# A two-block transformer kernel: the first block's activations are projected without the norm's factor per token

## The reference, cut to what matters

```
def rms_norm(x, g, eps=EPS):
    y = xf * lax.rsqrt(jnp.mean(xf * xf, axis=-1, keepdims=True) + eps)
    return y * g

h = rms_norm(x, norm_g[i])
proj = h @ w_in[i]
dq, dk, dv, dg, mq, mk, mv, mg, gates = split_in_proj(proj)
dq = partial_rope(dq, cos, sin);  dk, mq, mk likewise
o_a = diff_attention(dq, dk, dv, ...) * silu(dg)
o_b = moba_attention(mq, mk, mv) * silu(mg)
merged = sigmoid(g_a) * (o_a @ w_branch_diff) + sigmoid(g_b) * (o_b @ w_branch_moba)
```

## Time and profile before

| | |
|---|---|
| median of 3 runs | 1220.8 us (1220.32 to 1221.1) |
| the profiled execution's own time | 1220.15 us |
| its span (first to last instruction) | 1218.3 us |
| TensorE busy | 1186.1 us, 97% |
| VectorE, ScalarE, GpSimd busy | 911.3, 782.4, 417.3 us |
| mean granted TensorE clock | 0.997 of full |
| chain of waits by engine | PE 79%, POOL 9%, DVE 5%, issue 4%, ACT 3% |

### The profile page before, as it was taken

How to read it: one execution, slowest core, us unless ns; L and a number is a source line. 1 busy time by engine, 2 the same in 40 slices (tenths; PEclk the granted TensorE clock), 3 DMA queues, 4 the chain that set the end, 5 groups by cost and what they waited for, 6 DMA issues and landing times.

```text
span 1218.3 us, 26657 instructions
## 1 busy us (share of the span) xinstructions
PE 1186.1 (97%) x8256; PEld 1068.5 (88%) x8256; DVE 911.3 (75%) x1992; ACT 782.4 (64%) x1784; POOL 417.3 (34%) x398
## 2 busy tenths in 40 slices
PE   8999999999898999999999999999999999999997
PEld 8898988989787999888999999998888888888886
DVE  5788778889677769996788788851776768686766
ACT  5546676556775565667788878776655555555555
POOL 2230110011241049998777777789000000000000
PEclk9999999999999999999999999999999999999999
DMA  6787756549543446555666666667676676767663
GB/s 241 231 280 269 229 173 213 183 135 342 193 142 117 141 146 186 188 189 169 204 210 202 212 203 215 211 212 266 195 256 205 207 238 196 254 191 260 197 194 105
DMA packets 85829, 249.86 MB, mean 205 GB/s; under 512 B 8020, under 2 KB 29693, under 8 KB 84989
## 3 DMA queue, kind: packets, MB, share of 16 engines
q1 hardware_dynamic: 77356, 209.62, 54.3%
q0 software_dynamic: 8400, 39.34, 9.1%
HBM read 237.38 MB, written 13.12 MB: 206 GB/s over the span
## 4 chain that ended last, share of the span: by engine, by line
PE 79%; POOL 9%; DVE 5%; issue 4%; ACT 3%; POOLq 0%; DVEq 0%; ACTq 0%
PE psum L704 78%; POOL w_lo L1654 9%; DVE w_lo L1830 1%; ACT w_hi L1227 1%; PE psum L905 1%; ACT arena L1386 1%; DVE rstd L1824 1%; DVE h_parts L1879 0%; ACT arena L1210 0%; DVE arena L2044 0%; DVE arena L1950 0%; POOLq L1653 0%; ACT L1386 0%; DVE arena L2411 0%; DVE s_sb L1844 0%
## 5 line engine op out<-in xcount | busy, mean ns | idle before, releaser
L704 PE MATMUL psum<-h_parts,w_hi 128*128 128x256 f32 (+1 forms) x3216 | 673.9, 303 | 13.5 <-DVE h_parts L1879 4.4
L1227 ACT ACTIVATE w_hi<-ring 128x512 fp32r<-128x512 f32 x734 | 445.1, 627 | 247.9 <-PE psum L704 237.5
L704 PEld LDWEIGHTS psum<-h_parts,w_hi 128*128 128x128 f32 x3216 | 515.2, 191 | 47.5 <-issue 17.8
L704 PE MATMUL psum<-h_parts,w_lo 128*128 128x256 f32 x1832 | 517.1, 282 | 0.0
L1654 POOL TENSOR_TENSOR w_lo<-ring,w_hi 128x512 fp32r<-128x512 f32 x261 | 342.1, 1326 | 147.6 <-ACT w_hi L1227 139.2
L704 PEld LDWEIGHTS psum<-h_parts,w_lo 128*128 128x128 f32 x1832 | 349.9, 191 | 0.0
L704 PE MATMUL psum<-w_hi,h_parts 128*128 128x512 f32 (+1 forms) x1120 | 342.6, 388 | 0.2
L1830 DVE TENSOR_TENSOR w_lo<-ring,w_hi 128x512 fp32r<-128x512 f32 x345 | 229.3, 689 | 77.9 <-ACT w_hi L1227 77.3
L704 PEld LDWEIGHTS psum<-w_hi,h_parts 128*128 128x128 f32 x1120 | 208.6, 188 | 44.8 <-issue 3.0
L704 PE MATMUL psum<-w_lo,h_parts 128*128 128x512 f32 (+1 forms) x560 | 216.4, 386 | 0.0
L2362 DVE TENSOR_TENSOR w_lo<-ring,w_hi 128x512 fp32r<-128x512 f32 x128 | 88.5, 692 | 61.6 <-ACT w_hi L1227 58.1
(11 more groups left out here) (214 smaller groups left out, 1001.8 us busy)
## 6 DMA issues: line engine op xcount, KB each, us to landing
ring<-u_t SPq DMA_DIRECT2D x128, 512.0 KB, 3.6
ring<-v_rows SPq DMA_DIRECT2D x128, 512.0 KB, 4.2
ring<-weights SPq DMA_DIRECT2D x115, 512.0 KB, 4.3
arena<-mods POOLq DMA_DIRECT2D x48, 512.0 KB, 5.6
routing_weights<-s_sb SPq DMA_DIRECT2D x32, 320.0 KB, 4.2
s_sb<-routing_weights POOLq DMA_DIRECT2D x5, 2048.0 KB, 10.0
bias_rows<-bias_row POOLq DMA_DIRECT2D x1, 1536.0 KB, 11.2
xres<-x_t SPq DMA_DIRECT2D x2, 512.0 KB, 4.6
```

Of the source, the lines that this page charges most:

```text
L704: return nc.tensor.matmul(out, lhs, rhs, start=start, stop=stop, **kw)
L1227: nc.scalar.activation(w_hi[:, half, :], src, ACT.Copy).then_inc(hi_done, 1)
```

## The change

The activation parts are now made from x * gain alone, without rstd. So they need neither the sum of squares nor the reciprocal. Everything that is linear in the token's factor takes it later:

- **Start.** SP first issues a DMA for the 8 columns of norm gains, then x. VectorE makes `h_hi` of chunks 0 to 3 (a tensor_scalar) and `h_lo` of all 8 (scalar_tensor_tensor: x * gain - h_hi); ScalarE makes `h_hi` of chunks 4 to 7, after all four halves of `w_hi`. VectorE now also makes `w_lo` of dq1's first half, which GpSimd did. The 14 matmuls of ones after the sum are gone. TensorE does dq0 and dq1 by halves: dq0 over chunks 0 to 3, dq1 over 0 to 3, dq0 over 4 to 7, dq1 over 4 to 7.
- **Rotation.** VectorE multiplies cos and sin by rstd once; GpSimd's cos products wait for that.
- **Values.** Tokens are on partitions there, so the factor is needed as a column: at dv TensorE turns rstd with two matmuls (128 x 128 stationary, one column moving), VectorE copies the two columns out, and the four evictions become tensor_scalar with that column.
- **Gates.** GpSimd multiplies each of the 24 gate blocks by rstd in place, one block behind the projection; ScalarE's silu and sigmoid wait for it.

```diff
+            gains = slice(*PAR["norm_g"])
+            sp.dma_start(par[:, gains], params[:, gains]).then_inc(gain_in, 16)
             for i in range(2):
                 sp.dma_start(xres[:, 4 * i:4 * i + 4, :], x_t[:, 4 * i:4 * i + 4, :]).then_inc(x_in[i], 16)
...
                         sum_squares(AT[s + ("ssq",)], blk(SQ, 8), KC, lambda c: pe_.wait_ge(squared, c + 1))
-                        for _ in range(14):
-                            mm(psum[:, 7, 0:P], ones[:, :], ones[:, :], True, True)
...
+                    if s[1] == "dv":
+                        pe_.wait_ge(rstd_ready, 1)
+                        for i in range(TT):
+                            last = mm(psum[:, 7, T + i:T + i + 1], rstd[:, P * i:P * i + P], ident[:, 0:1], True, True)
+                        last.then_inc(token_done, 1)
...
-                    if s[1] in ("dq0", "nq0"):
+                    if s[1] == "dq0":
+                        outs, k = [take_a(AT[s] + j) for j in range(2)], SPLIT[SLOT_AT[s]]
+                        for b in range(2):
+                            for j in range(2):
+                                half = half_ready(k + j, b)
+                                for c in range(4 * b, 4 * b + 4):
+                                    pe_.wait_ge(h_ready, c + 1)
+                                    last = split_mms(outs[j], half, c % 4 * P, (h_hi[:, c, :], h_lo[:, c, :]), c == 0, c == KC - 1)
+                                last.then_inc(a_done if b else half_used, 1)
...
                     if k == 0:
-                        highs(0)
+                        highs(1)
+                        act.wait_ge(gain_in, 16)
+                        for c in range(DVE_PARTS, KC):
+                            nc.scalar.activation(h_hi[:, c, :], xres[:, c, :], ACT.Copy, scale=pcol("norm_g", c))\
+                                .then_inc(late_hi, 1)
...
+            def scale_gate(b):
+                pool.wait_ge(a_read, filled("proj", FILL1[b]))
+                dst = blk(SIL + b) if b < 8 else blk(SIG + b - 8)
+                nc.gpsimd.tensor_tensor(dst, dst, rstd[:, :], ALU.mult).then_inc(gate_scaled, 1)
...
                 while k_lo <= ahead(s):
-                    if k_lo == 1:
-                        pool.wait_ge(lo0_done, 1)
-                        low(1, 2, ring[:, 1, 0:HSLOT], 3, lo0_done)
                     second_half(k_lo)
                     k_lo += 1
+                if kind == "proj" and s[1] in FILL1[1:]:
+                    scale_gate(FILL1.index(s[1]) - 1)
+                elif kind == "ple":
+                    scale_gate(len(FILL1) - 1)
...
+            def low_start(c):
+                v.scalar_tensor_tensor(h_lo[:, c, :], xres[:, c, :], pcol("norm_g", c), h_hi[:, c, :].bitcast(F32),
+                                       ALU.mult, ALU.subtract).then_inc(h_ready, 1)
...
                     if k == 0:
-                        lows(0)
+                        dve.wait_ge(gain_in, 16)
+                        dve.wait_ge(x_in[0], 16)
+                        for c in range(DVE_PARTS + 1):
+                            if c == 4:
+                                dve.wait_ge(x_in[1], 16)
+                            if c < DVE_PARTS:
+                                v.tensor_scalar(h_hi[:, c, :], xres[:, c, :], pcol("norm_g", c), None, ALU.mult)\
+                                    .then_inc(start_hi, 1)
+                            if c:
+                                dve.wait_ge(start_hi, c)
+                                low_start(c - 1)
+                        low(0, ring[:, 0, 0:HSLOT], 1, lo0_done)
+                        low(2, ring[:, 1, 0:HSLOT], 3, lo0_done)
+                        k_lo = 2
+                        for c in range(DVE_PARTS, KC):
+                            dve.wait_ge(late_hi, c - DVE_PARTS + 1)
+                            low_start(c)
...
+                            dve.wait_ge(small_in, 16 * 8)
+                            for table in (cos_t, sin_t):
+                                v.tensor_tensor(table, table, rstd[:, :], ALU.mult).then_inc(table_scaled, 1)
+                            dve.wait_ge(table_scaled, 2)
...
+                    if s[1] == "dv":
+                        dve.wait_ge(token_done, 1)
+                        v.tensor_copy(token_rstd, psum[:, 7, T:T + TT]).then_inc(token_ready, 1)
+                        dve.wait_ge(token_ready, 1)
                     for i in range(TT):
                         n = VT[s + (i,)]
                         dve.wait_ge(v_done, n + 1)
-                        v.tensor_copy(rows[:, i, :], vbank(n)).then_inc(v_read, 1)
+                        v.tensor_scalar(rows[:, i, :], vbank(n), token_rstd[:, i:i + 1], None, ALU.mult).then_inc(v_read, 1)
```

More of the change, by code:

```diff
@@ L62 @@
 V_MODS = 4
+DVE_PARTS = 4
 MODS_A, MODS_O, MODS_B, MODS_C = 23, 26, 34, 40
@@ L282, in block_program @@
         gain_sum = blk(OT)
+        token_rstd = small[:, 48:48 + TT]
         gain_sq, gain_both = small[:, 32:40], small[:, 40:48]
@@ L376, in block_program @@
         th_done = sem("th_done")
+        gain_in = sem("gain_in")
+        start_hi = sem("start_hi")
+        late_hi = sem("late_hi")
+        table_scaled = sem("table_scaled")
+        token_done = sem("token_done")
+        token_ready = sem("token_ready")
+        gate_scaled = sem("gate_scaled")
         part_hi = sem("part_hi")
@@ L618, in _ @@
             load_slot(1)
-            sp.dma_start(par[:, :], params).then_inc(par_in, 16)
+            sp.dma_start(par[:, gains.stop:NPAR], params[:, gains.stop:NPAR]).then_inc(par_in, 16)
             for name, dst in (("ident", ident[:, :]), ("iota", iota[:, :]), ("valid", valid[:, :]),
@@ L1332, in _ @@
                     highs(ahead(s))
-                    first = {0: 0, 2: 8, 3: 16}[k]
-                    for c in range(KC):
+                    first = {0: 0, 2: 0, 3: 8}[k]
+                    for c in range(KC if k else 0):
                         act.wait_ge(t_ready, first + c + 1)
-                        if c == 0 and k:
+                        if c == 0:
                             act.wait_ge(*((a_done, filled("gate", 7)) if k == 2 else (v_done, VT["out2", 7] + 1)))
-                        t = blk(NTMP[k] + c)
-                        if k:
-                            sh = (0 if k == 2 else 24) + c
-                            nc.scalar.activation(h_hi[:, c, :], t, ACT.Identity, bias=mod[:, sh:sh + 1]).then_inc(th_done, 1)
-                        else:
-                            nc.scalar.activation(h_hi[:, c, :], t, ACT.Copy).then_inc(th_done, 1)
+                        sh = (0 if k == 2 else 24) + c
+                        nc.scalar.activation(h_hi[:, c, :], blk(NTMP[k] + c), ACT.Identity, bias=mod[:, sh:sh + 1])\
+                            .then_inc(th_done, 1)
                 elif s == ("x1", 0):
@@ L1940, in _ @@
                         if k == 0:
+                            dve.wait_ge(small_in, 16 * 8)
+                            for table in (cos_t, sin_t):
+                                v.tensor_tensor(table, table, rstd[:, :], ALU.mult).then_inc(table_scaled, 1)
+                            dve.wait_ge(table_scaled, 2)
                             dve.wait_ge(par_in, 16)
-                            k_lo = 2
                         lows(ahead(s))
-                    first = {0: 0, 2: 8, 3: 16}[k]
-                    for c in range(KC + 1):
+                    first = {0: 0, 2: 0, 3: 8}[k]
+                    for c in range(KC + 1 if k else 0):
                         if c < KC:
                             t = blk(NTMP[k] + c)
-                            gain = {0: pcol("norm_g", c), 2: gain_both[:, c:c + 1], 3: gm[:, 1, c:c + 1]}[k]
+                            gain = {2: gain_both[:, c:c + 1], 3: gm[:, 1, c:c + 1]}[k]
                             src = blk(MERGED + c) if k == 2 else xres[:, c, :]
```

18 lines of the change are left out of this document (9 added, 9 removed).

## The result

The changed kernel is slower, not faster. Its median is 1223.95 us (7 runs, 1222.69 to 1226.13) against 1220.8 us before; the ratio is 1.0023 (95% interval 1.0014 to 1.0032). Its profiled execution took 1223.29 us with a span of 1221.4, 3.1 us more than before. Forecast were 1217.1 us and a ratio under 1.

The account below looks back on a forecast made before the run. TensorE, busy 97% of the span, bounds the kernel, with waits at the start. Start -4.5, turning matmuls +0.45, evictions 0, gate products +0.4 sum to -3.65 us: 1217.1 us, forecast 1216.0 to 1218.4 (8-in-10 range 1215.0 to 1219.8).

Parts of the forecast that it names:

- step 4 of the start: Start: VectorE's first w_lo done at 9.57 us, squares summed by 9.4, so dq0 starts at about 9.65 instead of 13.85.
- the start's gain: Start up to dq2: dq2 begins at 17.3 to 17.8 us instead of 22.00, 4.5 us earlier, bounds 3.4 and 5.3.
- Step 1: Start: SyncE's one added DMA issue costs 0.45 us, so x lands at 5.4 us.
- Only about 0.3 us lie between the sum and dq0: Start: TensorE's remaining wait after the sum of squares, so the 14 removed matmuls of ones are not needed.
- The gate products: 24 products on GpSimd hold up VectorE, unhidden only at the attention stage's end: +0.4 us, bounds 0 and 2.2.
- A hold of that size is hidden there: Attention stage, 97 to 117 us: VectorE held 0.2 us, at most 0.74, by a gate product costs TensorE nothing.
- The slower rival: Attention stage, 97 to 188 us: gate products set VectorE's pace, 0.3 us each, 7.2 in all, so 1224; chance 6%.
- The clock rival: At 188.99 us: gates lengthen TensorE's 1.56 us wait to 2 and the clock falls, +1.5, so 1218.7; chance 6%.
- the value evictions: Behind the start: four evictions become tensor_scalar, difference 0, bounds -0.3 to +0.3 us in all.
- the turning matmuls: At dv: two added matmuls on a full TensorE, +0.45 us, bounds 0.25 and 0.93.
- VectorE's and GpSimd's hold on each other: Start, step 5: one GpSimd instruction holds VectorE up to 1.0 us; late h_lo end at 13.9, reciprocal starts then.
- the point to compare at: dq2's start, 22.00 us before: what it gains, everything behind inherits unless a new wait gives it back.

Follow-up runs that it names:

- a1: After, with norm 0's sum of squares in a PSUM bank of its own: 1219.85 us, ratio 0.9989 to the kernel before.
- a4: After, with the sum of squares in its own bank and 8 matmuls of ones before ple's third block: 1218.34 us, ratio 0.9977.
- a2: After without the 24 gate products on GpSimd: 1221.18 us, ratio 0.9995 to the kernel before.
- a3: After, with 8 matmuls of ones while TensorE waits for ple's third projection: 1222.06 us, ratio 0.9998.
- c2: After, with 11 matmuls of ones ahead of dq0: 1222.11 us, ratio 1.0008 to the kernel before.
- c1: a4 with all 24 gate products kept but moved three blocks later, the last four into ple: 1217.64 us, ratio 0.9968.
- b1: After, with 22 matmuls of ones ahead of dq0: 1224.19 us, ratio 1.0017 to the kernel before.
- after: The changed kernel itself, as first measured against the kernel before: 1223.95 us, ratio 1.0023.
- d1: After timed once more, unedited, beside d2: 1223.24 us, ratio 1.0010 to the kernel before.
- c4: c1 with the gain's columns loaded by GpSimd's queue instead of ahead of x on SyncE's: 1217.31 us, ratio 0.9974.
- b2: a4 without the 24 gate products: 1217.33 us, ratio 0.997 to the kernel before.
- d2: After, with 11 matmuls of ones ahead of dq0 and 8 at ple's third block: 1221.19 us, ratio 0.9998.
- b4: The kernel before, with 8 matmuls of ones at ple and 12 in the wait at 324 us: 1221.62 us, ratio 0.9999.

## Why the prediction was wrong

Both signs that were to show the forecast wrong are there: dq2 starts past 18.5 us, and the shift shrinks between 97 and 175 us.

**The step that failed is step 4 of the start**, "dq0 can start at about 9.65". It counted the operands of the first matmul and not its output. dq0 takes both PSUM buffers at once (`outs, k = [take_a(AT[s] + j) for j in range(2)]`), and `take_a` waits until the buffer's last content has been read. dq1's is the bank in which the squares were summed, and its reader is ScalarE's root, which the change moved behind the splits of both slots and four `h_hi`, to 12.24. The diff shows both edits. That halved the start's gain, 2.4 of 4.5 us; a1 and a4 show it by giving the bank back, and with it dq0 and dq2 come out to 0.2 us. Step 1 was off on its own: the gain's DMA cost x 0.75 us, not 0.45.

**"Only about 0.3 us lie between the sum and dq0"** failed with it. It became 2.86 us of idle TensorE, with the 14 matmuls of ones gone that had kept it busy there, and in some executions the clock fell (a2, a3). What that costs the changed kernel in the median is not shown (c2).

**The gate products** cost 1.0 to 1.1 us, inside the bounds of 0 to 2.2 but not +0.4. "A hold of that size is hidden there" was wrong at one place: products beside VectorE's softmax work at 96 to 100 us made a `w_lo` late, and TensorE waited for it at 103.40 (0.5 us). The loss at the end of the stage was placed rightly. The slower rival's 1224 is the measured median, and that is luck: it had this mechanism with a price of 0.3 us for every product, 7.2 in all, on a start of full size. The products cost 1.0 to 1.1 in all, and c1 shows that most cost nothing.

**The clock rival came true**, at the place and by the cause that it named: the wait rose above 2 us (2.21), and the clock fell. It was priced at 1.5, from a window that began 0.4 us into the fall, and was 1.69; I gave it 6%. It does not come in every execution (b1). Worse, I let it stand alone. The rival does not exclude the others: the same holds that cost 0.67 us lengthen the wait that costs 1.69. With the start halved as well, -3.65 becomes -2.12 + 0.23 + 0.13 + 1.06 + 1.69 + 0.16 = +1.15. The longer fall at 330 us (+0.85) is in after and d1, and in a1, a2, b1, c1, c2 and c4, with or without a fall at "ple"; the kernel before, a4, b2 and d2 have the short one, a3 none. The traces show what goes with its length: in the eight with the longer fall the clock fell while TensorE was still idle (after: at 328.7 us, idle until 329.92; c1: 323.7, idle until 325.08), in the four with the shorter one it fell after TensorE had begun again (before: 329.6, idle until 328.77; a4: 327.2, idle until 325.97). What sets that moment, and so whether an edit brings the one or the other, stays open. The last +1.1 is scatter of the run's later part, which d1 doesn't have and b4 does.

**What held:** the value evictions (at most 0.13), the turning matmuls within their bounds (0.23 against 0.45, at the lower one), VectorE's and GpSimd's hold on each other, and the point to compare at.

## What to carry to other kernels

A matmul waits for its output bank as well as for its operands: when a reader is moved back in its engine's row, ask which buffer it sets free. Where one addition lengthens a wait of TensorE that is near the length behind which the clock has fallen elsewhere in the trace, price the fall as a consequence of the addition and not as a case apart. An operation that holds VectorE is cheap or dear by where it stands: moving it three blocks back gave what leaving it out gave.
